# Seven expert-row buffers and five weight blocks in place of eight and four, in a two-model transformer kernel on one Trainium2 core

## What is computed

```python
def chunk(xc):                                   # 128 tokens
    q = (xc @ w_query).reshape(PEER_CHUNK, PEER_HEADS, 2, half)
    s = jnp.einsum('thpk,pnk->thpn', q, sub_keys)
    sv, si = lax.top_k(s, PEER_TOPK)             # 16 of 128 keys, for either half
    ...
    top_s, sel = lax.top_k(cand, PEER_TOPK)      # 16 of 256 pairs
    eidx = jnp.take_along_axis(cidx, sel, axis=-1)
    g = jax.nn.softmax(top_s, axis=-1)
    u = expert_down[eidx]
    vv = expert_up[eidx]
    act = jax.nn.gelu(jnp.einsum('td,thkd->thk', xc, u), approximate=False)
    return jnp.einsum('thk,thkd->td', (g * act), vv)
```

## Time and profile before

| | |
|---|---|
| median of 3 runs | 2647.95 us (2647.44 to 2648.21) |
| the profiled execution: its own time | 2646.2 us |
| its span in the profile | 2644.3 us |
| PE busy | 2479.8 us, 94% |
| DVE busy | 1475.5 us, 56% |
| ACT busy | 935.1 us, 35% |
| POOL busy | 593.3 us, 22% |
| moved by DMA | 817.47 MB, mean 309 GB/s |
| ring block loads, expert row gathers | 252, 512 |
| chain that ended last: PE, DMA, DVE | 58%, 21%, 14% |

### The profile page before, as it was taken

One profiled execution on the slowest core, in us unless ns is written; L12 is line 12 of the kernel. 1 busy time (PEld: TensorE's weight loads), 2 busy tenths in 40 slices (PEclk: granted clock), 3 DMA queues, 4 the chain that ended last, 5 costly groups with the idle time before them and its releaser, 6 DMA issues.

```text
span 2644.3 us, 29500 instructions
## 1 busy us (share of the span) xinstructions
PE 2479.8 (94%) x9800; PEld 1691.8 (64%) x9800; DVE 1475.5 (56%) x3170; ACT 935.1 (35%) x2311; POOL 593.3 (22%) x600
## 2 busy tenths in 40 slices
PE   8999999988888989999998989999889999999999
PEld 6668655533444536677555555567357888878888
DVE  3623686899877636424877777777758200182000
ACT  2351354435544322432444445432446200062000
POOL 0000333333444410001333333333423000030000
PEclk9999999999999999999999999999999999999999
DMA  7575999999999994657999999999993344423444
GB/s 280 177 281 180 411 418 427 421 395 411 403 427 427 424 369 167 229 219 289 404 427 426 427 427 419 426 426 425 419 368 112 135 152 157 161 102 137 159 146 157
DMA packets 113647, 817.47 MB, mean 309 GB/s; under 512 B 12432, under 2 KB 14528, under 8 KB 14944
## 3 DMA queue, kind: packets, MB, share of 16 engines
q0 software_dynamic: 75136, 549.29, 49.8%
q1 hardware_dynamic: 38368, 266.35, 27.2%
HBM read 814.54 MB, written 1.05 MB: 308 GB/s over the span
## 4 chain that ended last, share of the span: by engine, by line
PE 58%; DMA 21%; DVE 14%; issue 3%; ACT 3%; POOL 1%; ACTq 0%; DVEq 0%; SPq 0%; POOLq 0%
PE work L672 41%; DMA arena<-experts,arena 20%; PE acc L672 16%; DVE arena L2052 4%; DVE arena L1841 3%; POOL arena L638 1%; PE work L764 1%; DVE small L1841 1%; ACT L1515 1%; DVE arena L2000 1%; DVE arena L2001 1%; DVE arena L2003 1%; ACT arena L1525 0%; DVE arena L2002 0%; DVE arena L1999 0%
## 5 line engine op out<-in xcount | busy, mean ns | idle before, releaser
L672 PE MATMUL acc<-arena 128*128 128x512 f32 (+1 forms) x1900 | 881.2, 612 | 130.2 <-ACT arena L1525 126.6
L672 PE MATMUL work<-arena,ring 128*128 128x256 f32 (+2 forms) x3396 | 736.7, 378 | 3.6 <-DVE arena L2236 2.0
L638 POOL DMA_INDIRECT arena<-experts,arena x512 | 530.0, 1035 | 891.0 <-PE acc L672 716.9
L672 PEld LDWEIGHTS acc<-arena 128*128 128x128 f32 (+1 forms) x1900 | 356.8, 195 | 557.9 <-issue 350.0
L672 PEld LDWEIGHTS work<-arena,ring 128*128 128x128 f32 x3396 | 641.0, 190 | 103.1 <-issue 14.0
L2052 DVE SCALAR_TENSOR_TENSOR arena<-arena,h 128x1024 f32<-128x1024 f32 x256 | 311.5, 1225 | 175.4 <-DMA arena<-experts,arena 172.4
L2052 DVE SCALAR_TENSOR_TENSOR arena<-arena,acc 128x1024 f32<-128x1024 f32 x256 | 308.2, 1220 | 150.6 <-DMA arena<-experts,arena 147.4
L672 PE MATMUL work<-h,ring 128*128 128x256 f32 (+1 forms) x1440 | 325.6, 379 | 1.7 <-DMA ring<-stream 1.0
L672 PEld LDWEIGHTS work<-h,ring 128*128 128x128 f32 x1440 | 266.9, 191 | 69.9 <-issue 36.7
L1515 ACT ACTIVATE arena<-arena 128x2 f32<-128x2 f32 x258 | 52.4, 203 | 613.0 <-DVE arena L2052 612.1
L672 PE MATMUL work<-lent,ring 128*128 128x256 f32 x992 | 224.3, 379 | 0.0
(11 more groups left out here) (265 smaller groups left out, 1888.0 us busy)
## 6 DMA issues: line engine op xcount, KB each, us to landing
ring<-stream SPq DMA_DIRECT2D x252, 1024.0 KB, 5.1
arena<-experts,arena POOLq DMA_INDIRECT x512, 12.3
arena<-na_bias POOLq DMA_DIRECT2D x2, 2048.0 KB, 15.1
arena<-consts POOLq DMA_DIRECT2D x1, 2304.0 KB, 14.0
lent<-consts POOLq DMA_DIRECT2D x2, 1024.0 KB, 8.2
arena<-consts POOLq DMA_DIRECT2D x1, 1816.0 KB, 19.0
x<-x_in SPq DMA_DIRECT2D x1, 1024.0 KB, 5.6
xc<-ctx_in POOLq DMA_DIRECT2D x1, 1024.0 KB, 11.0
```

The source lines that it names most:

```text
L638: pool.indirect_dma_start(rows[:, m % ROWS, :], None, experts[l], bass.IndirectOffsetOnAxis(ap=expert[:, n:n + 1], axis=0))\
L672: ins = nc.tensor.matmul(o, w, r, start=start, stop=stop, **kw)
```

## The change

`RING` goes from 4 to 5 and `ROWS` from 8 to 7. Both kinds of buffer hold 8 KB per partition, so the ring grows by what the arena loses (`ARENA`, 30960 to 28912 numbers). What lay behind `rows` moves forward by one buffer; the constants `c2` of the second model stay where they were, now by a number of their own (`c2_at`). The number of held-back releases follows `RING`, and so does the slot from which they are passed on: from pick 251 on before, from pick 250 on now. The stream is padded to a multiple of `RING` blocks: 252 blocks before, of which 2 are padding, and 250 now, none.

```diff
-RING = 4
+RING = 5
...
-ROWS = 8
+ROWS = 7
...
-ARENA = 30960
+ARENA = 28912
...
-        assert used[0] <= lent_at
+        c2_at = 8 * 2 * D
         sq_part2 = rs2[:, 0, :]
-        c2 = arena[:, lent_at:lent_at + C2_N]
-        used[0] = lent_at + C2_N
+        c2 = arena[:, c2_at:c2_at + C2_N]
+        used[0] = c2_at + C2_N
...
                 def slot(n):
-                    if PICKS - 5 <= n < PICKS - 1:
+                    if PICKS - 1 - RING <= n < PICKS - 1:
                         owed.append(kept.pop(0))
```

## The result

The change made the kernel slower by more than I had forecast: **2667.44 us** in the median (2665.44 to 2671.26, four runs) against 2648.08 us for the kernel before, a ratio of 1.0076 with a 95% interval of 1.0063 to 1.0089. That is +19.4 us where the sum said +6.1. The direction was right; the time lies above my range and within 2 us of the third rival. The profiled execution of the changed kernel took 2671.26 us (span 2669.3 us). It is the slowest of the four, and 25.1 us slower than the profiled execution of before (2646.2 us): differences between the two traces are to be held against these 25.1 us.

What follows compares the result with a forecast made beforehand. Bytes were taken to set the pace inside the two gather loops and PE outside. Terms 5.2 - 0.4 - 1.0 + 4.8 - 2.5 gave +6.1 us on 2646.2, 2652.3, plus 1.75 to the median: 2654.0 us, range 2645 to 2664.

Steps and rivals of the forecast that it cites:

- the sum: Whole kernel: 5.2 - 0.4 - 1.0 + 4.8 - 2.5 = +6.1 us; the forecast built on it kept a chance of 0.45.
- the third rival: Gather loops: the queue runs thin everywhere, half a microsecond per gather in three windows, +18 us, 2666 us; chance 0.12.
- the first paragraph: Bound: bytes inside the gather loops, PE outside; at 528 to 594 us consumers, with all eight buffers holding landed rows.
- What one row buffer less costs: Gather loops: gathers issued when their successors were come late at five places, together +5.2 us; other gathers keep more.
- the 6.2 us: Gather loops: time a row needs between its successor's issue and its own old landing, middle of 5.6 and 6.8 us.
- named places: Layer 0 at 356, 530, 662 us, layer 1 at 1277, 1634 us: losses of 1.3, 0.3, 2.1, 0.9, 0.6 us.
- The fifth block inside the loops: One ring load per layer drops out of each gather loop: -0.4 us in layer 0, -1.0 us in layer 1.
- The end of the loops: Last gathers of each layer: one more block under way beside the last rows, +2.4 us per layer, +4.8 us.
- The start of layer 1: PE waits for ring blocks 2.5 + 0.7 us there; the fifth block is fetched in the gap before: -2.5 us.
- my four terms for it: Fifth ring block: -0.4 and -1.0 us inside the loops, +4.8 us at their ends, -2.5 us at layer 1's start.
- The first (only bytes count): Gather loops and ring waits: cover is long enough, saved loads and waits gain 7.4 us, 2640.5 us; chance 0.13.
- The second (it cancels): Gather loops: PE's work in hand absorbs late rows, ring gains pay for last rows, within 2 us of 2648; chance 0.30.

Runs made afterwards that it cites:

- the short runs: Kernel before, with 141 gathers (picks 8-40, 86-150, 234-244, 264-286, 396-404) also waiting as if there were seven row buffers: 2664.80 us, +16.8 us.
- the extra wait at 45: Kernel before, with the 45 gathers within four of picks 32, 94, 144, 274, 400 also waiting as if there were seven row buffers: 2655.21 us, +7.2 us.
- the extra wait: Kernel before, with gathers also waiting until the buffer of the pick seven before is free; for all 504 gathers: 2672.65 us, +24.6 us.
- the 363: Kernel before, with only the gathers outside the 141 of the short runs also waiting as if there were seven row buffers: 2657.05 us, +9.0 us.
- four blocks, nine rows (shared tables): Kernel before with a ninth row buffer, room made by small tables sharing memory: 2642.21 us, ratio 0.9975.
- run 71: No run number: 71 counts landings; "that run" is the kernel before with the extra wait for the other 363 gathers only, 2657.05 us.
- the pair with eight row buffers: Small tables sharing memory, eight row buffers: five ring blocks 2644.11 us, against four ring blocks 2647.25 us.
- layout control: Kernel before, still four ring blocks and eight row buffers, but with small tables sharing memory: 2647.25 us, ratio 0.9999.

## Why the prediction was wrong

**The bound was read rightly.** Of the 25.1 us between the profiled executions 23.5 lie in the two gather loops. One reading of the first paragraph was wrong: that at 528 to 594 us all eight buffers hold landed rows. In the trace of before at least one gather is under way at every moment of that stretch, and for all but 0.6 us two or more.

**The step that failed is "What one row buffer less costs", in its last sentence: "Other gathers keep more".** The term was +5.2 us; the lost row buffer alone measured +18.2. I took the shortest landings as the places where time is short, looked at five pairs of gathers, and closed the list. Counted over the trace of before, 61 gathers keep less than the 6.2 us that I held to be needed, and what they lack adds up to 58 us. (That sum is no price either: the short runs that hold nearly all of them cost 16.8 us. That a late row makes the next ones late with it, so that the same lateness is counted again, would account for it, but is not shown.) They come in runs. One long run, for which I had listed no place, is layer 0 at 608 to 656 us in the kernel before:

```profile
L638 POOL DMA_INDIRECT arena<-experts,arena x18: 933/937/1668, 609.5 to 654.8; - x18
...
DMA to landing us min/median/max: 7.1/8.3/10.7
```

No single landing here is as short as the 5.6 us of the earlier trace rows. But the median is 8.3 us, and less one row of 2.46 us that leaves 5.8. Of these eighteen gathers fourteen keep less than 6.2 us, most of them by little. My own, a median of 8.6 us in 1254 to 1320 us, said the same of layer 1. I used it for the third rival alone, and I set that aside because rows that lie landed cost nothing when late.

**The size of the named places** was of the right order: 5.2 us forecast for five gathers, 7.2 us measured with the extra wait at 45. No run held the five alone, and the extra wait costs somewhat more than a missing buffer (24.6 against 18.2 us in full). The rest was lost in two parts that the term had at nothing: 9.6 us at other gathers of the short runs, and 9.0 us at the 363 that nearly all keep more than 6.2 us. So the second failure is the 6.2 us itself, taken as a line above which a gather loses nothing.

**What stands in place of my 6.2 us.** I had assumed a time that a gather needs, below which it is late. The traces show the pace of the landings going with how many gathers are under way. I went over every landing (rows and ring blocks) of both loops, from 40 us after a loop's first issue to 20 us before its last landing, some 520 in each run, and sorted the time to the next landing by the number of gathers still under way:

| kernel | landings with two gathers or fewer left | mean time to the next | with more than two left | beyond 2.46 us, in all |
|---|---|---|---|---|
| four blocks, nine rows (shared tables) | 11 | 2.96 us | 2.49 us | 5.5 us |
| before | 28 | 2.97 us | 2.49 us | 14.2 us |
| four blocks, seven rows | 75 | 3.00 us | 2.47 us | 40.3 us |
| the change | 79 | 2.99 us | 2.47 us | 42.1 us |
| five blocks, six rows | 247 | 3.06 us | 2.47 us | 148.1 us |

The last column is the first count times what the mean exceeds 2.46 us by. Whatever the number of buffers, a landing follows after 2.47 to 2.49 us in the mean while three or more gathers are under way, and about half a microsecond later otherwise. What the buffers change is how often that happens. The cut between two and three is mine, and the traces show no step there: in the kernel before, the next landing comes after 2.99 us with two left, 2.70 with three, 2.58 with four and 2.30 with five.

The differences of the last column against before (-9, +26, +28, +134 us) follow the measured ones (-5.9, +18.2, +19.4, +123 us), and are larger. The other landings make up for most of that: with six or seven buffers they come 0.01 to 0.02 us closer together than with eight, some 275 to 450 times. With both kinds counted the differences are -5, +17, +22 and +124 us. That sum is nearly the length of the loops itself, so it must agree with the times; what the table adds is which landings the loss lies at.

It does not explain the 363 gathers. In the profiled execution of that run 71 landings have two or fewer left, at 2.93 us in the mean, which makes 33.3 us in the last column, 19 more than before; the execution took 2650.23 us, 4.0 more than the profiled one of before. The number under way is thus a sign of the loss and no price for it, and why those gathers cost 9.0 us in the median stays open. The table is a count over five executions and goes with the times; no run here set the number under way directly.

**The fifth block inside the loops** (-0.4 and -1.0 us): the two gains are seen at picks 216 and 462, and both are gone a dozen picks later. With rows as the limit, a load less lets DMA run ahead only until it wants a free buffer, as the step said. Four blocks and five cost the same with seven row buffers, within the noise.

**The end of the loops** (+4.8 us) was too high. With eight row buffers the last gathers took 2.2 and 1.1 us longer, with seven 1.7 and 1.4 us (12.6 and 12.6 against 10.9 and 11.2 in the run with four blocks). I had also expected over 15 us for the last gather of layer 0, and it took 12.6, less than the 15.7 of before: with seven buffers four rows are under way when it is issued, where it was five, and I had left that out. One row is 2.46 us; from 15.7 to the 10.9 us of seven rows and four blocks it is 4.8, so the rest of this stays open. The Trainium skill, DMA: Bandwidth & Descriptors, section "Queues, rings and completion order", has each DMA engine go round between its queues packet by packet; the 2.2 us of layer 0 are near the full row that I had drawn from it, the 1.1 us of layer 1 are not.

**The start of layer 1** (-2.5 us): 3.0 us less waiting for ring blocks, as forecast, in the pair with eight row buffers. In the changed kernel itself PE's ring waits at 960 to 1030 us are down to 0.4 us, but no time was gained by it: a wait for DVE stands in their place, and from the last landing of layer 0 to the first gather of layer 1 it took 267.1 us after 267.3.

```profile
PE work L672 <- DVE h L1841: 2.4, 1, 2.4
PE acc L672 <- DMA ring<-stream: 0.4, 1, 0.4
```

With eight row buffers the fifth block is worth -3.1 us in all, where my four terms for it sum to +0.9.

**The rivals.** The first (only bytes count) is refuted: a median landing far above the bare time protects nothing when one gather in eight (61 of 512) keeps less than it needs. The second (it cancels) too. The third was right that the queue runs thin at many gathers, and I had held against it that DVE is the bound in two of its three windows. The slices there fell all the same, by 9 to 14 GB/s. That its time of 2666 us came out so near is luck: it put its 18 us into those three windows, but the picks issued in them in the kernel before (92 to 115, 142 to 167, 264 to 288) make 3.7 of the 25 us by which the last row lands later in the changed kernel's trace, 5 of 18 with seven rows and four blocks. Most of the loss lay elsewhere. Its half microsecond for each gather is not what was seen either: 0.12 us for each gather in the short runs. The Trainium skill's fixed 2.0 us plus bytes at 436 GB/s, 4.4 us for such a row (same page, "Anatomy of one DMA — SWDGE (gpsimd) path"), would have made the sum about -0.6 us. The shortest landing of the changed kernel is 5.5 us. It is a gather that was issued with nothing else under way (two later ones were issued before it landed). It and the measured +19.4 us stand against the rule:

```profile
L638 POOL DMA_INDIRECT arena<-experts,arena x1: 936/936/936, 687.2 to 687.2; - x1
...
DMA to landing us min/median/max: 5.5/5.5/5.5
```

**PE's clock** may be part of the loss, and I had no term for it. PE's busy time rose by 7.6 us (2479.8 to 2487.4) for the same 9800 matmuls, the mean `acc` matmul from 612 to 615 ns. In the stretch from 528 us on the granted clock was 0.93 after 0.97, and in the run with six buffers 0.87, where PE waits more. But PE's busy time in a single profiled execution scatters as much. The layout control has 2487.4 us too, a granted clock of 0.92 in that stretch and 0.984 over its span (0.988 before, 0.986 in the changed kernel), and took no longer than the kernel before. So no part of the 19 us is shown to be clock, and how much is stays open.

## What to carry to other kernels

Where transfers set the pace, a buffer is worth what it adds to the queue, and its worth is steep: here 5 us for the ninth, 18 to 19 for the eighth, 103 for the seventh. Don't judge the cover by the shortest landing or by the median over all, but by the median landing in each stretch less one transfer time. Count every gather that falls below, not the few extremes, and don't take those above for free: here they were 9 of the 25 us. And when two buffers are traded, run each half of the trade alone: here one half gained 3 us and the other lost 18. The halves need not add up: together they lost 19, so with seven row buffers the 3 us were not seen.

## What the runs showed of the hardware

- In the two gather loops the next 1 MB transfer (a row or a ring block) lands 2.46 to 2.49 us after the one before, in the mean, when three or more gathers are under way, and 2.84 to 3.14 us after it when two or fewer are, in all fourteen profiled executions. The change is gradual: with exactly three it is 2.57 to 2.75 us.
- DMA's busy share hardly shows this; the GB/s line is the one to read. The run with six row buffers has a share of 0.96 at 371 GB/s, and the kernel before has 1.01 at 427 at 1452 us, but at the start of layer 1:

```profile
1254.00:1320.00 66.00, 64.60 (x202) 37.46 (x201) 59.79 (x156) 30.61 (x78) 24.06 (x25) 0.98 1.00 404
```

  The share is 1.00 at 404 GB/s.

- An always fulfilled wait ahead of each of POOL's gathers costs no time at the end that can be told from nothing (+1.8 us in the median, interval -1.9 to +2.9), even though 503 were added.
